# The low parts of a weight tile's two halves: one VectorE operation of 2048 columns in place of two of 1024

## The reference, cut to what matters

```python
for i in range(DEPTH):                 # mixers: mLSTM, windowed attention, 2-D attention, mLSTM
    hc = rmsnorm(xc) * (1 + mod[1]) + mod[0]        # the same for xl
    xc = xc + mod[2] * mixer_i(hc)                  # projections, scan or attention, projection
    hc = rmsnorm(xc) * (1 + mod[4]) + mod[3]
    u = dwconv(hc @ w_up)                           # 1024 -> 5632
    xc = xc + mod[5] * ((silu(u[:, :2816]) * u[:, 2816:]) @ w_down)
```

## Time and profile before

| | |
|---|---|
| time, median of 3 runs | 1853.03 us (1852.29 to 1854.17) |
| profiled execution: time | 1852.1 us |
| profiled execution: span of the trace | 1850.3 us |
| PE busy | 1800.3 us (97%) |
| PEld busy | 1497.0 us (81%) |
| DVE busy | 1388.4 us (75%), 2064 instructions |
| ACT busy | 986.9 us (53%) |
| POOL busy | 176.2 us (10%) |
| mean granted TensorE clock | 0.994 of full speed |

### The profile page before, as it was taken

The page is one execution under the profiler, slowest core; times in us unless marked ns, Lnnn a source line. Parts: engine busy times, 40 slices in busy tenths (PEclk is TensorE's granted clock), DMA queues, the critical chain, the costliest instruction groups (busy, mean ns, idle before and its releaser), DMA issues.

```text
span 1850.3 us, 27379 instructions
## 1 busy us (share of the span) xinstructions
PE 1800.3 (97%) x11032; PEld 1497.0 (81%) x11032; DVE 1388.4 (75%) x2064; ACT 986.9 (53%) x1492; POOL 176.2 (10%) x147
## 2 busy tenths in 40 slices
PE   5999999999999999999999999999999999999998
PEld 2988877798888867888977778888888787878888
DVE  3865677668998766999865588988765777769984
ACT  2754444545674454766345466744654445547763
POOL 2100121001000113000101110002100210020001
PEclk8999999999999999999999999999999999999999
DMA  9565656867666767675584776566555645445542
GB/s 368 194 230 197 210 208 226 317 232 278 260 218 215 288 229 273 251 290 194 211 304 169 295 290 275 204 226 257 213 196 175 230 178 213 176 166 200 195 175 84
DMA packets 74175, 421.28 MB, mean 228 GB/s; under 512 B 12384, under 2 KB 18936, under 8 KB 26432
## 3 DMA queue, kind: packets, MB, share of 16 engines
q1 hardware_dynamic: 55440, 392.98, 57.1%
q10 hardware_dynamic: 18608, 26.55, 4.3%
HBM read 408.51 MB, written 10.96 MB: 227 GB/s over the span
## 4 chain that ended last, share of the span: by engine, by line
PE 88%; DVE 6%; issue 2%; ACT 2%; POOL 1%; DMA 1%; POOLq 0%; DVEq 0%; ACTq 0%; SPq 0%
PE ps L652 18%; PE ps L674 9%; PE ps L709 9%; PE ps L655 9%; PE ps L634 6%; PE ps L690 5%; PE ps L712 4%; PE ps L637 3%; PE ps L620 3%; PE ps L753 3%; PE ps L622 3%; PE ps L621 3%; PE ps L960 1%; PE ps L723 1%; PE ps L722 1%
## 5 line engine op out<-in xcount | busy, mean ns | idle before, releaser
L498 DVE TENSOR_TENSOR spl_lo<-raw,spl_hi 128x1024 fp32r<-128x1024 f32 x556 | 690.8, 1268 | 149.6 <-ACT spl_hi L487 148.6
L487 ACT ACTIVATE spl_hi<-raw 128x1024 fp32r<-128x1024 f32 x556 | 574.0, 1053 | 288.0 <-PE ps L712 109.5
L652 PE MATMUL ps<-H,spl_hi 128*128 128x512 f32 x1408 | 444.3, 397 | 4.9 <-DVE H L1849 3.6
L655 PEld LDWEIGHTS ps<-H,spl_lo 128*128 128x128 f32 x1408 | 264.5, 188 | 62.4
L655 PE MATMUL ps<-H,spl_lo 128*128 128x256 f32 x1408 | 276.8, 278 | 0.0
L652 PEld LDWEIGHTS ps<-H,spl_hi 128*128 128x128 f32 x1408 | 214.3, 189 | 19.3 <-issue 16.5
L709 PE MATMUL ps<-G,spl_hi 128*128 128x512 f32 x528 | 165.8, 395 | 0.0
L634 PE MATMUL ps<-B,spl_hi 128*128 128x512 f32 x512 | 160.8, 395 | 0.0
L620 PE MATMUL ps<-H,spl_hi 128*128 128x256 f32 x512 | 149.0, 291 | 5.7 <-DVE H L1854 3.1
L621 PE MATMUL ps<-H,spl_hi 128*128 128x256 f32 x512 | 145.8, 285 | 0.0
L622 PE MATMUL ps<-H,spl_lo 128*128 128x256 f32 x512 | 145.8, 285 | 0.0
(11 more groups left out here) (255 smaller groups left out, 2944.4 us busy)
## 6 DMA issues: line engine op xcount, KB each, us to landing
raw<-in_stream SPq DMA_DIRECT2D x366, 1024.0 KB, 4.9
out_new_C<-c_stage ACTq DMA_DIRECT2D x16, 512.0 KB, 3.8
column<-in_ada_cols SPq DMA_DIRECT2D x16, 512.0 KB, 4.6
ada_b<-in_ada_b ACTq DMA_DIRECT2D x4, 768.0 KB, 9.3
cond_all<-cond_out ACTq DMA_DIRECT2D x3, 1024.0 KB, 7.4
E<-rows_out ACTq DMA_DIRECT2D x8, 256.0 KB, 4.3
Em<-rows_out ACTq DMA_DIRECT2D x8, 256.0 KB, 4.6
x<-in_x ACTq DMA_DIRECT2D x1, 1024.0 KB, 11.8
```

The costliest lines, as they stand in the source:

```text
L487: act.activation(spl_hi[m % SPL][:, :], raw[r % RAW][:, h * HALF:(h + 1) * HALF], ACT.Copy).then_inc(S["hi_done"], 1)
L498: dve.tensor_tensor(spl_lo[m % SPL][:, :], raw[r % RAW][:, h * HALF:(h + 1) * HALF], spl_hi[m % SPL][:, :].bitcast(F32), ALU.subtract).the ...
L652: pe.matmul(banks[:, b * 512:(b + 1) * 512], spl_hi[m % SPL][:, c], H[:, kk * 512:(kk + 1) * 512], start=kk == 0, stop=False, skip_group_c ...
L655: mm = pe.matmul(banks[:, b * 512:b * 512 + TOK], spl_lo[m % SPL][:, c], H[:, kk * 512:kk * 512 + TOK], start=False, stop=kk == KD - 1, sk ...
```

## The change

`split_lo` with both halves now waits until both high parts are there, makes the low parts of the whole tile in one operation of 2048 columns, and raises `lo_done` by 2 at its end. With one half it is as before. The buffers stay where they were in memory; two neighbouring half buffers get a common name, so that one operation can span them.

```diff
-    spl_hi = [sb(f"spl_hi{r}", HALF, F32R, 32 * KB + 4 * KB * r) for r in range(SPL)]
-    spl_lo = [sb(f"spl_lo{r}", HALF, F32R, 48 * KB + 4 * KB * r) for r in range(SPL)]
+    hi_pair = [sb(f"spl_hi{r}", TILE, F32R, 32 * KB + 8 * KB * r) for r in range(SPL // 2)]
+    lo_pair = [sb(f"spl_lo{r}", TILE, F32R, 48 * KB + 8 * KB * r) for r in range(SPL // 2)]
+    spl_hi, spl_lo = ([pair[r // 2][:, HALF * (r % 2):HALF * (r % 2 + 1)] for r in range(SPL)] for pair in (hi_pair, lo_pair))
...
         r = POS[MAIN[n]]
+        if len(halves) == 2:
+            dve.wait_ge(S["hi_done"], 2 * n + 2)
+            dve.tensor_tensor(lo_pair[n % 2][:, :], raw[r % RAW][:, :], hi_pair[n % 2][:, :].bitcast(F32),
+                              ALU.subtract).then_inc(S["lo_done"], 2)
+            return
         for h in halves:
             m = 2 * n + h
             dve.wait_ge(S["hi_done"], m + 1)
```

## The result

The changed kernel takes 1891.78 us (median of 4 runs, 1890.51 to 1895.04), the kernel before 1853.6 beside it: a ratio of 1.021, with an interval of 1.0194 to 1.0227. The change costs some 38 us. The forecast was 1885, range 1867 to 1894; the result lies at the upper edge of the forecast's own range (1877 to 1892).

A forecast was written before the change was run, and what follows sets the result against it. The prediction took TensorE (busy 97% of the span) as the bound, so each late half tile counts. Stalls of 7.1 + 13.6 + 4.05 + 2.6 + 5.0 = 32.4 us on 1852.1 gave 1884.5, predicted as 1885 us, range 1867 to 1894.

The forecast's parts named there:

- (a): Loop of ml_x over two tiles, two layers: each of six turns 1.19 us longer, 7.1 us.
- (b): Ten second tiles of stages (eight behind a norm, two of ml_down): TensorE stalls for the later first half, 13.6 us.
- (c): Heads of layer 3: ml_z tiles come later, part is hidden by a later wait, 4.05 us stay.
- (d): Gates' scan in layers 0 and 3: later splits delay TensorE's load by 1.2 and 1.4 us, 2.6 us.
- No gap absorbs it: Gates' scan, layer 0: the split at 123.61 pushes all else on VectorE up to the next split by 0.87 us.
- (e): Single places: layer 1's queries, layer 0's second value tile, attention in layers 1 and 2, four layer 3 splits; 5.0 us.
- on the chain there, 0.87: Split before the first softmax sums in layer 1: on the chain, so it costs 0.87 us.
- The gain taken as nothing: Pair beside GpSimd's sum of squares, layers 1 and 2: one operation ends 1.1 us sooner, hidden by the norm, 0.
- Stalls given back: Rival: TensorE's stalls are partly given back, 17 us remain, 1870 us; 13 in 100.
- GpSimd late at all nine norms: Rival: GpSimd's sums of squares sit out longer operations before all nine norms, 9.6 us on top, 1894; 12 in 100.
- VectorE's time counts: Rival: the instruction's fixed cost is on every tile's path, 190 x 0.06 = 11 us faster, 1842; 3 in 100.
- the one I weighed: Skill's rule: some 60 ns overhead per VectorE instruction, larger operations help if saturated; alone 11 us back, not adopted.

The follow-up runs named there:

- Experiment 1: The kernel before, with the single operation only at tiles 2 to 7 of ml_x in layers 0 and 3 (12 of 190 tiles): 1860.32 us, ratio 1.0038.
- experiment 4: The changed kernel, with the ten second tiles of stages kept in two operations: 1876.05 us, ratio 1.0125 to the kernel before.
- experiment 5: The changed kernel, with twelve tiles (gates' scan of layers 0 and 3, heads of layer 3) again in two operations: 1883.59 us, ratio 1.0169 to the kernel before.
- experiment 9: The changed kernel, with only tile 99 (first of layer 1's output projection) in two operations: 1889.17 us, ratio 1.0199 to the kernel before.
- experiment 10: The kernel before, with 119 tiles in one operation and the ml_x loop's first half in two pieces of 512 columns: 1850.41 us, ratio 0.999.
- experiment 6: The changed kernel's single operation only at the 125 tiles where no loss was found, 65 left in two: 1854.68 us, ratio 1.0016 to the kernel before.
- experiment 8: The kernel before, with one operation only at the first ffn_up tile of layers 1 and 2: 1853.27 us, ratio 1.0002.
- Experiment 7: The kernel before, with the first half's low part in the ml_x loop made in two pieces of 512 columns, TensorE starting on the first: 1851.03 us, ratio 0.9992.

## Why the prediction was right, and where it fell short

**The frame held.** Slower, for the reason named: the first half of a tile comes 1.1 to 2.0 us later, and VectorE's saved time (0.06 us a pair back to back, 25 us in all) falls where nothing waits for it. Experiment 1 puts a price on the loop alone (8 us), experiments 4, 5 and 9 take others back place by place (16, 8 and 3 us), and experiment 10 shows that 119 of the other merges are neutral.

**(a), (b), (c), (d)** are right within 0.3, 1.4, 0.35 and 0.6 us. In (b) the 0.2 us taken off for a load that runs ahead wasn't there: TensorE's load follows 0.05 us behind the low part (450.93 + 2.29 = 453.22, load at 453.27), and the later `ffn_up` tiles lost 0.2 us more than forecast (1.55 against 1.34 at the last). In (d) the size was near, the way was not: I took the second half of the scan (tile 14) to be 1.2 late. It was 0.48, and 1.03 came at tile 12, by way of ScalarE, which I had not followed. "No gap absorbs it" was said of VectorE alone.

**(e) is the step that was mis-sized**: 5.0 forecast, 9.1 measured. For tile 99 I took "on the chain there, 0.87"; it was 2.48, and behind tile 137 came 1.65 us that I had at nothing. In both places TensorE did the same work at half its clock for 3.4 us; no term of my sum held the clock. These two make 3.3 of the 6.2 us that the sum lacked. The clock also gave something back: the kernel before has it at half from 1070.67 to 1074.09, ahead of tile 152, the changed kernel not, and that is some 1.1 us of the 1.88 gained there (layer 1, without such a fall, gained 0.74). The rest is 1.4 in (b), 1.3 in the small steps, 0.8 in smaller singles, and less elsewhere. So that the time came out inside the forecast's own range is in part luck: which falls of the clock a run has was in no term.

**The gain taken as nothing** (102 and 151) was -1.0 us net. Without the clock's part it was nothing, +0.07 us in layer 1. The mechanism was as described: VectorE's operation takes 2.28 us there, not 3.46, and GpSimd's sum 3.28, not 2.22.

**The rivals.** *Stalls given back*: no. Only 1.2 us in the heads and 2.6 at the ends of the attention came back; the first was in the sum, and 1.1 of the second is the clock. *GpSimd late at all nine norms*: the stall is real, GpSimd is busy 14.7 us longer, but in the changed kernel it surfaces at no norm as a step of its own; experiments 6 and 8 see it at two. The time came near that rival's 1894 by another road. *VectorE's time counts*: refuted by experiment 6, where 16.6 us less of it gave nothing (I had expected 8 us less: 0.06 us a tile was too little for the whole saving, as said above). The Trainium skill ("Perfetto Trace Analysis", section "Optimizing Scalar/DVE Operations") has a second sentence that fits better than the one I weighed: "If Scalar/Vector aren't saturated, but are causing bubbles on other engines, breaking up instructions may allow work to be completed sooner." Experiment 7 agrees with it, 0.4 to 0.5 us a turn.

**What stays open** is how far a single fall of the clock belongs to the change. All three traces with tile 99 in one operation have one there (the changed kernel, experiments 4 and 5), and no other trace has. Of the three with tile 137 in one operation, two have one (the changed kernel and experiment 9); experiment 5, with the same wait, doesn't. Others came and went between kernels that are alike there. What decides it isn't shown.

## What to carry to other kernels

Before you join two operations, ask who waits for the first: the price is the second's length plus the time until its input is ready, less the consumer's slack, at each place, and the saving is one fixed cost (here 0.06 us against 1.1 to 2.0). Join where the slack is larger, split where the consumer waits, and count slack again for each choice, since a neighbour's operation can be the cover. Follow a late engine through every engine that reads from it, not only down its own queue.

## What the runs showed of the hardware

- A wait of TensorE can cost twice, but doesn't always. After a wait of 2.72 us (2.94 busy us in 5.20) the granted clock was 0.50 for 3.4 us, which was worth 1.65 us; after the same wait in another kernel (2.71 us, 2.95 busy us in 5.20) it stayed at 1.00. At a second place a fall of the same length was worth some 1.4 us.
- VectorE's subtraction and GpSimd's addition, both on two inputs in SBUF, don't overlap: whichever came second was done only 1.1 to 1.2 us after the first had ended, behind a half as behind a whole tile. So the length of one operation sets the other engine's delay: GpSimd's sum took 1.27 us at the first norm (20.10), 2.21 behind a half and 3.26 behind a whole tile.
- Two places shift by 1.1 to 1.2 us between executions, for reasons that aren't the change's, and no step below that size there may be read as its effect. At tile 61 ScalarE waits for the raw tile (0.18 us before, 1.58 in experiment 7). At tile 25 the raw tile landed 18 us ahead (185.67, high part at 203.92); there the issue of a load on ScalarE took 1.55 us in one execution and 0.48 in another.
